# Moving four modulation weight units into spare places, splitting the opening loads in half units, and giving two units to GpSimd and ScalarE

## The reference

```python
c_act = jax.nn.silu(c)                         # c: 1 x 1024
mod = c_act @ ada_w[l] + ada_b[l]              # ada_w[l]: 1024 x 6144
shift_m, scale_m, gate_m, shift_f, scale_f, gate_f = jnp.split(mod, N_MOD, axis=-1)
h = rms_norm(x, g_pre_mix[l]) * (1.0 + scale_m) + shift_m
proj = h @ w_in[l] + b_in[l]
...                                            # attention, pooling
x = x + gate_m * rms_norm(mix @ w_out[l], g_post_mix[l])
h = rms_norm(x, g_pre_ffn[l]) * (1.0 + scale_f) + shift_f
x = x + gate_f * rms_norm(ffn(h), g_post_ffn[l])
```

## Time and profile before

| | us |
|---|---|
| median of 3 runs | 1170.61 (1170.38 to 1171.25) |
| the profiled execution | 1170.48 |
| its span | 1168.5 |
| PE busy | 1140.9 |
| DVE busy | 811.5 |
| ACT busy | 628.0 |
| POOL busy | 29.0 |

### The profile page before, as it was taken

The page is one execution under the profiler, slowest core; times in us unless marked ns, Lnnn a source line. Parts: engine busy times, 40 slices in busy tenths (PEclk is TensorE's granted clock), DMA queues, the critical chain, the costliest instruction groups (busy, mean ns, idle before and its releaser), DMA issues.

```text
span 1168.5 us, 19588 instructions
## 1 busy us (share of the span) xinstructions
PE 1140.9 (98%) x7862; PEld 1020.5 (87%) x7862; DVE 811.5 (69%) x1258; ACT 628.0 (54%) x1113; POOL 29.0 (2%) x68
## 2 busy tenths in 40 slices
PE   7999999999999999999999999999999999999997
PEld 4556999999887999999899899999989889999996
DVE  6698988776998756645677667656656866766653
ACT  3077544445566544445666766445556676655443
POOL 3100000000000000000000000000000000000000
PEclk9999999999999999999999999999999999999999
DMA  9995998887445866556343546555534435555530
GB/s 361 413 378 220 355 365 329 319 334 268 189 164 198 319 231 225 210 190 238 128 181 109 180 174 217 180 183 183 187 139 156 145 132 195 196 186 194 181 109 37
DMA packets 37996, 254.04 MB, mean 217 GB/s; under 512 B 4537, under 2 KB 4881, under 8 KB 9874
## 3 DMA queue, kind: packets, MB, share of 16 engines
q1 hardware_dynamic: 35138, 243.95, 56.6%
q0 software_dynamic: 2624, 8.84, 2.1%
q10 hardware_dynamic: 144, 0.00, 0.0%
HBM read 251.69 MB, written 1.08 MB: 216 GB/s over the span
## 4 chain that ended last, share of the span: by engine, by line
PE 86%; DVE 6%; ACT 3%; DMA 3%; issue 1%; SPq 0%; DVEq 0%; ACTq 0%
PE bank L497 26%; PE bank L499 25%; PE bank L498 25%; PE bank L504 3%; DMA raw_w<-weights 2%; DVE raw_w L1641 2%; PE bank L546 2%; PE bank L595 2%; ACT gtok L1173 1%; DVE lo_w L1628 1%; DMA shared<-bias_rows 1%; PE bank L946 1%; DVE tok L1853 0%; PE bank L638 0%; PE bank L897 0%
## 5 line engine op out<-in xcount | busy, mean ns | idle before, releaser
L1628 DVE TENSOR_TENSOR lo_w<-raw_w,hi_w 128x1024 fp32r<-128x1024 f32 (+3 forms) x346 | 409.4, 1209 | 122.7 <-ACT hi_w L1168 122.3
L1168 ACT ACTIVATE hi_w<-raw_w 128x1024 fp32r<-128x1024 f32 (+3 forms) x346 | 350.6, 1040 | 103.9 <-PE bank L499 89.2
L497 PE MATMUL bank<-in_hi,lo_w 128*128 128x256 f32 x1408 | 396.0, 281 | 0.0
L499 PE MATMUL bank<-in_hi,hi_w 128*128 128x256 f32 x1408 | 392.8, 279 | 0.0
L498 PE MATMUL bank<-in_lo,hi_w 128*128 128x256 f32 x1408 | 392.8, 279 | 0.0
L497 PEld LDWEIGHTS bank<-in_hi,lo_w 128*128 128x128 f32 x1408 | 264.3, 188 | 2.6 <-issue 0.8
L498 PEld LDWEIGHTS bank<-in_lo,hi_w 128*128 128x128 f32 x1408 | 263.7, 187 | 1.9 <-issue 0.5
L499 PEld LDWEIGHTS bank<-in_hi,hi_w 128*128 128x128 f32 x1408 | 264.7, 188 | 0.0
L497 PE MATMUL bank<-hi_w,hid_lo 128*128 128x512 f32 x352 | 139.6, 396 | 0.2 <-DVE hid_lo L2116 0.2
L498 PE MATMUL bank<-lo_w,hid_hi 128*128 128x512 f32 x352 | 139.0, 395 | 0.0
L499 PE MATMUL bank<-hi_w,hid_hi 128*128 128x512 f32 x352 | 139.0, 395 | 0.0
(11 more groups left out here) (227 smaller groups left out, 1141.1 us busy)
## 6 DMA issues: line engine op xcount, KB each, us to landing
raw_w<-weights SPq DMA_DIRECT2D x213, 1024.0 KB, 4.9
ink<-ink_w SPq DMA_DIRECT2D x8, 640.0 KB, 13.9
rows<-mod_rows POOLq DMA_DIRECT2D x7, 512.0 KB, 6.9
rows<-norm_rows POOLq DMA_DIRECT2D x5, 512.0 KB, 4.9
raw_w<-weights SPq DMA_DIRECT2D x4, 512.0 KB, 8.9
ink<-whole_w SPq DMA_DIRECT2D x2, 1024.0 KB, 22.2
early_out<-whole_w SPq DMA_DIRECT2D x2, 1024.0 KB, 7.6
raw_w<-weights SPq DMA_DIRECT2D x2, 832.0 KB, 4.5
```

The source lines that it names most:

```text
L497: nc.tensor.matmul(o, st[1], mv[0], start=start, stop=False, **kw)
L499: return nc.tensor.matmul(o, st[0], mv[0], start=False, stop=stop, **kw)
L1168: nc.scalar.activation(hi_w[:, m % NSPLIT, cut], raw_view(unit)[:, cut], ACT.Identity).then_inc(*sig("hi_w", unit, i))
L1628: nc.vector.tensor_tensor(lo_w[:, m % NSPLIT, cut], raw_view(unit)[:, cut], hi_w[:, m % NSPLIT, cut].bitcast(F32), ALU.subtract).then_inc( ...
```

## The change

Seven edits, all in layer 0's opening (up to about 110 us), but for renamed semaphores.

1. The entries n0 to n7 are loaded in halves: for each feature tile t, two half units (512 KB each) and then `ink[t]`. VectorE works tile by tile. The vector table `vrow` is loaded ahead of them.
2. ScalarE applies silu to c's one row ahead of the broadcast on TensorE, and then copies the broadcast.
3. POOL loads the bias behind unit 5 and not behind unit 7.
4. n12 to n15 go to spare places in `ink`, where the input weights k = 0 to 7 have been used; n16 to n19 take `raw_w`'s places behind n8 to n11. `whole[0]` and `whole[1]` are loaded behind n17 and n18, and not behind n13 and n15.
5. Units 12 and 13 (n16, n17) are multiplied by GpSimd (four instructions of 128 x 1024), and ScalarE sums each product along the row. VectorE leaves them out, and moves its other units one place later: unit 8 stood among the `evacuate`s.
6. The scores use banks 5, 6, 7, 2, 3, 4, and the turned probabilities another order of banks; `shares(3)` goes ahead of `exps(4)`, and `shares(4)` ahead of `exps(5)`.
7. The scale row is spread behind the attention's part of w_out, beside the shift row, and ScalarE copies the shift row behind `x_root(0)`.

```diff
+SPARE = {12 + _i: _i for _i in range(4)}
+BY_POOL = (("ada", 0, 12), ("ada", 0, 13))
-WHOLE_AFTER = {("ada", 0, 9): 2, ("ada", 0, 10): 3, ("ada", 0, 17): 0, ("ada", 0, 19): 1}
+WHOLE_AFTER = {("ada", 0, 9): 2, ("ada", 0, 10): 3, ("ada", 0, 13): 0, ("ada", 0, 14): 1}
...
+        spare = [ink[:, NSPLIT * SLOT * w + SLOT * i:][:, 0:SLOT] for w in range(2) for i in range(2)]
...
                     banks(4, 5, 6, 7)
+                    spread_row(L, "scale", 1)
                     spread_row(L, "shift", 1)
...
-                    banks(4, 5, 6, 7, 2, 3)
+                    banks(5, 6, 7, 2, 3, 4)
                     scores_late()
...
-                    banks(0, 1, 4, 0, 1, *((6, 5, 7, 4) * 4))
+                    banks(0, 1, 5, 0, 1, *((7, 6, 5, 4) * 4))
...
                     spread_row(L, "gate", 0)
-                    spread_row(L, "scale", 1)
                 attention(0)
...
+            for t in range(KT):
+                tiles_in(t, (lambda n: f"tile_in{TILE_IN[n]}") if t % 2 == 0 else (lambda n: f"raw_w{n % NRAW}"))
+                sp.dma_start(ink[t], a_ink[t, :, :]).then_inc(*sig(f"ink_in{t}", by=16))
...
+                    if n in SPARE:
+                        sp.wait_ge(*(due("ink_used", 3) if SPARE[n] < 2 else due("in", 0, 1, 2)))
+                        sp.wait_ge(*due(f"raw_w{n % NRAW}", old))
+                    elif n - NRAW in SPARE:
+                        sp.wait_ge(*due(f"raw_w{n % NRAW}", old))
+                        sp.wait_ge(*due("ada", UNITS[n - 2 * NRAW][0]))
+                    else:
+                        sp.wait_ge(*due(*(("summed", old, 1) if old in BY_POOL else ("ada", old) if old[0] == "ada" else ("lo_w", old, 1))))
...
             angles()
+            pool.wait_ge(*due("ada", ("ada", 0, 5)))
+            load(bias, a_bias[0:1, :], 1280, "bias_in", 0)
             pool.wait_ge(*due("ada", ("ada", 0, 7)))
-            load(bias, a_bias[0:1, :], 1280, "bias_in", 0)
...
+            pool.wait_ge(*due("c_act", 1))
+            for unit in BY_POOL:
+                pool.wait_ge(*due(f"raw_w{UNIT_NO[unit] % NRAW}", unit))
+                for f in range(2):
+                    w = raw_view(unit)[:, D * f:D * (f + 1)]
+                    nc.gpsimd.tensor_tensor(w, w, c_row[:, :], ALU.mult).then_inc(*sig("pool_made", unit, f))
...
                 y_root(0)
                 if (L, w) == (0, 0):
+                    row_in(0, "scale", 1)
+                x_root(0)
+                if (L, w) == (0, 0):
                     row_in(0, "shift", 1)
-                x_root(0)
...
+                def sums(unit):
+                    for f in range(2):
+                        sc.wait_ge(*due("pool_made", unit, f))
+                        w, at = raw_view(unit)[:, D * f:D * (f + 1)], 2 * unit[2] + f
+                        nc.scalar.activation(w, w, ACT.Identity, accum_out=mods[:, 0, at:at + 1]).then_inc(*sig("summed", unit, f))
...
                     row_in(0, "gate", 0)
-                    row_in(0, "scale", 1)
+                    sums(BY_POOL[0])
                     for jp in range(2):
                         copy(("attn", 0, jp), raw[:, 2 * jp:2 * jp + 2, :].rearrange("p t s -> p (t s)"), ps(("attn", 0, jp))[:, :], "attn_cat", 0, jp)
+                    sums(BY_POOL[1])
                     prepare(("gu", 0, 0))
...
+                    if (l, n) == (0, 15):
+                        ve.wait_ge(*due("summed", BY_POOL[-1], 1))
```

More of the change, by code:

```diff
@@ L987, in _ @@
             pe.wait_ge(*due("ve_step", 1))
-            pe.wait_ge(*due("c_in", 0))
+            pe.wait_ge(*due("c_act", "row"))
             for c in range(2):
@@ L1038, in _ @@
                     sp.dma_start(whole[u].rearrange("p t c -> p (t c)"), a_whole[u, :, :]).then_inc(*sig(f"whole_in{u}", by=16))
-                for kk in INK_AFTER.get(unit, ()):
-                    sp.dma_start(ink[kk], a_ink[kk, :, :]).then_inc(*sig(f"ink_in{kk}", by=16))
             for T in range(2):
@@ L1822, in started @@
                 scale, shift = (modcol[:, ROWS[(0, kind, 0)], :] for kind in ("scale", "shift"))
-                for tiles in ((0,), (1,), (2, 3), (4, 5), (6, 7)):
-                    j, a, b = tiles[0] // 2, tiles[0], tiles[-1] + 1
-                    if tiles == (0,):
-                        ve.wait_ge(*due("ada_first", ("ada", 0, 0)))
-                    elif tiles == (1,):
-                        ada_tile(0, 4, 1)
-                        ada_tile(0, 0, 1)
-                        ve.wait_ge(*due("ada", ("ada", 0, 0)))
-                    else:
-                        ada(0, 4 + j)
-                        ada(0, j)
+                for t in range(KT):
+                    j, f = t // 2, t % 2
+                    ada_tile(0, 4 + j, f)
+                    last = ada_tile(0, j, f)
+                    if f == 0:
+                        step(last)
+                    else:
@@ L1835, in started @@
                         ve.wait_ge(*due("ada", ("ada", 0, j)))
                     ve.wait_ge(*due("vcol", 0))
-                    mod_column(0, "shift", 0, 0, a, b, shift[:, a:b])
-                    step(mod_column(0, "scale", 0, 8, a, b, scale[:, a:b]))
-                    for t in tiles:
-                        for T in range(2):
-                            ve.wait_ge(*due("turned", T, t // 4))
-                        nc.vector.tensor_scalar(raw[:, t, :], raw[:, t, :], scale[:, t:t + 1], shift[:, t:t + 1], ALU.mult, ALU.add).then_inc(
-                            *sig("scaled0", t))
+                    mod_column(0, "shift", 0, 0, t, t + 1, shift[:, t:t + 1])
@@ L1845, in in_job @@
+                    step(mod_column(0, "scale", 0, 8, t, t + 1, scale[:, t:t + 1]))
+                    for T in range(2):
+                        ve.wait_ge(*due("turned", T, t // 4))
+                    nc.vector.tensor_scalar(raw[:, t, :], raw[:, t, :], scale[:, t:t + 1], shift[:, t:t + 1], ALU.mult, ALU.add).then_inc(*sig("scaled0", t))
             def in_job(L, T, c):
```

115 lines of the change are left out of this document (65 added, 50 removed).

## The result

| | us |
|---|---|
| median of 8 runs | 1174.07 (1173.22 to 1174.90) |
| before, 8 runs beside them | 1170.61 (1170.04 to 1171.38) |
| ratio | 1.0027, 95% interval 1.0018 to 1.0036 |
| the profiled execution | 1174.9, span 1172.8 |

A forecast was written before the change was run, and what follows sets the result against it. TensorE, busy 1140.9 of 1168.5 us, was taken as the bound, its feed-forward start in layer 0 setting the end. `lo` 1.9 later plus 0.3 behind it gave 2.2: 1170.6 + 2.2 = 1172.8 us, range 1167.9 to 1175.2.

The forecast's parts named there:

- The lock: Units 12 and 13: each GpSimd multiply blocks VectorE for 2.15 us, four cost 8.6, against 4.6 saved.
- The projection: Opening: k = 7 ready at 44.1, 9.1 us of work behind it, end at 53.2, first `scored` at 54.5, 2.4 earlier.
- VectorE's chain: Behind the softmax: free at 75.2, five units, two `mod_column`s and `lo`, plus 8.6 for multiplies: `lo` ends at 98.3.
- a predicted sign: TensorE waiting 3 to 4 us at the shift row's spread, at about 92.5, and 1 to 2 at the transposes.
- n20: Spare places, deeper issue: n20 lands between 89.7 and 92.9, taken as 90.7, before at 92.9.
- The swap of shares and the banks: Softmax and first scores: waits of 1.67 us and, at the fourth turned block, 1.41 us go, with 0.3 of small ones.
- The shift row behind the root: Behind `lo`: the copy ahead of the norm costs the first half 0.6 us; TensorE is 0.3 later in sum.
- The rival of a cheap GpSimd: VectorE unblocked or multiplies of 1.15 us: `lo` ends around 94.2, time 1168.9 (1167.7 to 1170.6); chance 0.3.
- Carried to the end unchanged: Whole kernel behind the opening: any shift of TensorE's start of layer 0's feed-forward reaches the end unchanged.

The follow-up runs named there:

- the two runs with scratch data: Changed kernel, VectorE doing all units, GpSimd making four unused 1024-column instructions: multiplies reading SBUF 1178.52 us, memsets only writing 1172.03 us.
- c_units_early_lo_late: Changed kernel without GpSimd's multiplies; fillers partly replaced by k = 6 slices, shift row ahead of root, units 12, 13 ahead of 17, `lo` behind scaling: 1170.10 us.
- c_vector_filler_shift: Changed kernel without GpSimd's multiplies, with three unused filler matmuls in the opening and the shift row copied ahead of the root: 1169.88 us, ratio 0.9991.
- c_hi_behind_root: As c_units_early_lo_late with three filler matmuls instead of slices, ScalarE rounding n20 behind the root and `lo` behind the norm: 1170.25 us, ratio 0.9994.
- a_gpsimd_writes_scratch: Changed kernel with VectorE doing all units, and four 1024-column memsets on GpSimd that nobody reads: 1172.03 us, ratio 1.0007.
- a_vector_only: Changed kernel with edit 5 taken back, VectorE multiplying and summing units 12 and 13 itself: 1172.12 us, ratio 1.0012.
- b_order_only: Kernel before with only edit 6, the order of banks, of unit 8 and of the shares: 1171.80 us, ratio 1.0005.
- a_filler_matmuls: Changed kernel plus three matmuls with unused results (the fillers) while TensorE waits for k = 6 and k = 7: 1174.02 us, ratio 1.0025.

## Why the prediction was right in its number, and where it was not

- **The lock: right, and its size too.** Predicted 8.6 us lost for four multiplies, 4.6 saved. The trace has 8.3, and of the two runs with scratch data the one that reads SBUF has it and the one that only writes has not. The Trainium skill's rule (SBUF — State Buffer, Who interferes with whom) is borne out here on VectorE's side too, where no row of before showed it. By the medians edit 5 costs 1.9 us in the changed kernel and 3.5 alone, there by another path than this sum.
- **The projection: the step that failed.** "The projection ends at 53.2" and "the first `scored` starts 54.5, 2.4 us earlier". The projection ended at 55.65 and `scored` started at 56.85. 1.5 of the missing 2.35 us are TensorE's clock, which fell to half behind the waits for k = 6 and k = 7; the fillers give them back. The other 0.8: k = 7 was ready at 44.7 and not at 44.1, and small waits. The sum counted idle TensorE as free, and priced what comes behind it at full clock; where the fillers kept the clock up, the 9.1 us that it gave to the work behind k = 7 came out (45.05 to 54.12).
- **VectorE's chain: the same sum, 2.3 us later.** It was to be free of the softmax at 75.2 with five units left; at 75.15 it only began unit 16, a sixth. So 98.3 became 100.15, 1.85 later than predicted; 1174.9, the profiled execution, is 2.1 above 1172.8. Against the median of 1174.07 the sum is off by 1.3: the number lies in the range although the gain of 2.4 us that it started from was not there.
- **The blocked reciprocal: not seen.** The first two blocked tiles stood ahead of the last reciprocal, and 2.65 us of TensorE's and 4.34 of ScalarE's waiting came of it. It cost nothing, as the run without it shows, since VectorE's tiles set the end. But it is why a predicted sign failed: there was no wait of 3 to 4 us at the shift row's spread, and 0.59 and not 1 to 2 at the transposes. TensorE was done with its own work at 105.25 and not at 98.9. Had `lo` ended at 98.3 as predicted, the normed half would have stood near 104, and TensorE would have been last.
- **n20: wrong, and off the path.** Predicted landing 90.7, it was 94.76, because its issue waits for ScalarE's sum of unit 12 (the DMA engines moved 16 GB/s at 86 to 88 us). `lo` began 3.1 us after that, when VectorE was free. With the issue out of the way (c_units_early_lo_late) it lands at 90.65, so the bytes were priced right.
- **The swap of shares and the banks: right.** TensorE's fifth turned block came 1.8 earlier (76.39 against 78.21), and edit 6 alone brings `scored` 1.9 forward.
- **The shift row behind the root: right in its part, and nothing at the end.** The norm waits 1.07 us, 0.54 more than the 0.53 before, and 0.6 were predicted. From `gain` to the first matmul it is 9.02 us against 8.97 before, where 0.3 more were predicted.
- **The rival of a cheap GpSimd: its price was wrong.** Without the lock I expected 1168.9; VectorE alone with all other edits gives 1172.1, and memsets on GpSimd beside it 1172.0. The other edits don't pay: the opening's gain of 2.4 us isn't there, n20's issue waits for unit 12, and what is won at the start shrinks later (next point). With the fillers, and the shift row moved back, it is 1169.9.
- **"Carried to the end unchanged": nearly true of the delay, not of a lead.** From trace to trace the start of the transposes of later norms is 3.5 to 3.8 late at 102, 560, 673 and 861 us of before, 3.5 at 973, and 4.3 at the last matmul. Leads shrink. That of c_vector_filler_shift is 1.3 at 296 us, 1.15 at 673, and 0.3 at 861 and 973; that of c_hi_behind_root 1.3, 1.3, 0.5 and 0.4; that of c_units_early_lo_late 1.6, 1.8, 0.9 and 0.9, and 0.1 at the last matmul. a_gpsimd_writes_scratch starts the feed-forward 0.2 us earlier than before, is 0.4 late at 861, and its profiled execution took 1171.67 against 1170.48. So some 0.8 us of a lead go between 673 and 861, in a stretch that no edit touches. From the mark at 973 to the end of the span, the profiled execution of before takes 195.4 us, the others 195.4 to 196.6. These are single executions, and what makes the difference stays open; but the sentence that all rests on holds to 1 us for the forecast delay and fails for a gain of 1 to 3 us.

Open as well: how much of the 1.0 us by which a_vector_only is slower than before is the clock, how much n20's landing, and how much the loss behind 673 us. No run takes back one of the edits 1 to 4 by itself.

## What to carry to other kernels

Before work goes to GpSimd beside a VectorE stretch of instructions with two SBUF inputs, price it as GpSimd's whole duration on VectorE, also for VectorE's tiny instructions; the memset, which doesn't read SBUF, was free here. A gap of 2 to 3 us on TensorE may not be free either: behind most of them here the work ran at half the clock, so price the work behind a new wait at both levels, and look for real work to fill it. And where several chains meet (bytes, VectorE, TensorE), work out for each edit which of them is last afterwards: b_order_only won 1.9 us at `scored`, a_filler_matmuls 1.5, and neither anything at the end. Last, when a stage is said to carry a shift to the end unchanged, compare its later marks in both traces: leads of 1 to 2 us were down to less than 1 at 861 us here.
